# Layer 0's first key and query tiles projected by quarters of 256 features, between the modulation slabs

## What is computed

```python
m_lat = (cond_lat @ mod_w[i] + mod_b[i]).reshape(bsz, N_MOD, 1, dm)
m_ctx = (cond_ctx @ mod_w[i] + mod_b[i]).reshape(N_MOD, dm)
h_lat = x_lat * (1.0 + m_lat[:, 1]) + m_lat[:, 0]
h_ctx = x_ctx * (1.0 + m_ctx[1]) + m_ctx[0]
q, k, v = jnp.split(h @ w_qkv, cuts, axis=-1)     # layer 0
```

## Time and profile before

| what | value |
|---|---|
| median of the three runs | 2414.4 us |
| span of the profiled execution | 2413.2 us |
| time of the profiled execution outside its span | not given; the span is 1.2 us under the median |
| TensorE matmul busy | 2340.2 us (97%) |
| first projection matmul starts | 43.28 us |
| matmul of tile 3 starts | 69.19 us |
| moved by DMA | 310.94 MB, mean 129 GB/s |

### The profile page before, as it was taken

One profiled execution on the slowest core, in us unless ns is written; L12 is line 12 of the kernel. 1 busy time (PEld: TensorE's weight loads), 2 busy tenths in 40 slices (PEclk: granted clock), 3 DMA queues, 4 the chain that ended last, 5 costly groups with the idle time before them and its releaser, 6 DMA issues.

```text
span 2413.2 us, 35782 instructions
## 1 busy us (share of the span) xinstructions
PE 2340.2 (97%) x13872; PEld 1903.1 (79%) x13872; DVE 1696.3 (70%) x2583; ACT 1129.2 (47%) x1948; POOL 335.6 (14%) x269
## 2 busy tenths in 40 slices
PE   6999999999999989999999999899999999989998
PEld 3765888888888559888879877788888889848998
DVE  3376689988444777999875236768999845487875
ACT  3466643442442576434324444455434325386663
POOL 0000311111110003111112003422111102002110
PEclk9999999999999999999999999999999999999999
DMA  8621645557233113555563421043555645404664
GB/s 260 204 71 39 215 142 164 166 148 208 81 97 92 30 58 100 166 157 166 162 180 86 113 70 45 2 132 114 166 163 158 192 116 125 129 13 123 187 180 132
DMA packets 449420, 310.94 MB, mean 129 GB/s; under 512 B 11922, under 2 KB 404674, under 8 KB 448996
## 3 DMA queue, kind: packets, MB, share of 16 engines
q1 hardware_dynamic: 446480, 307.09, 43.2%
q10 hardware_dynamic: 2772, 1.56, 0.2%
HBM read 307.56 MB, written 1.05 MB: 128 GB/s over the span
## 4 chain that ended last, share of the span: by engine, by line
PE 85%; DVE 6%; ACT 4%; issue 2%; DMA 2%; ACTq 0%; SPq 0%; DVEq 0%
PE bank L1690 74%; PE bank L1973 2%; DMA slab_raw<-in_mod_w 2%; PE bank L1993 1%; PE bank L2037 1%; ACT p L793 1%; DVE slab_lo L1047 1%; DVE stat L1316 1%; ACT hb L610 1%; DVE q_part L1375 1%; PE bank L1749 1%; PE bank L1768 1%; ACT slab_hi L595 1%; ACT pt L805 1%; PE bank L2165 1%
## 5 line engine op out<-in xcount | busy, mean ns | idle before, releaser
L1690 PE MATMUL bank<-h_hi,slab_hi 128*128 128x512 f32 (+1 forms) x2416 | 841.9, 348 | 4.1 <-DVE h_lo L1112 2.5
L1690 PE MATMUL bank<-h_hi,slab_lo 128*128 128x512 f32 (+1 forms) x2416 | 828.9, 343 | 0.0
L1690 PE MATMUL bank<-h_lo,slab_hi 128*128 128x512 f32 (+1 forms) x2416 | 828.9, 343 | 0.0
L1047 DVE TENSOR_TENSOR slab_lo<-slab_raw,slab_hi 128x1024 fp32r<-128x1024 f32 (+1 forms) x388 | 526.2, 1357 | 296.1 <-ACT slab_hi L595 294.8
L595 ACT ACTIVATE slab_hi<-slab_raw 128x1024 fp32r<-128x1024 f32 (+1 forms) x388 | 400.8, 1034 | 303.8 <-PE bank L1690 228.0
L1690 PEld LDWEIGHTS bank<-h_hi,slab_hi 128*128 128x128 f32 x2416 | 458.0, 190 | 85.6 <-issue 19.8
L1690 PEld LDWEIGHTS bank<-h_hi,slab_lo 128*128 128x128 f32 x2416 | 458.0, 190 | 53.8
L1690 PEld LDWEIGHTS bank<-h_lo,slab_hi 128*128 128x128 f32 x2416 | 458.3, 190 | 53.3 <-issue 0.5
L1021 ACT ACTIVATE conv<-bank,prm 128x512 f32<-128x512 f32 (+1 forms) x176 | 127.7, 725 | 446.6 <-PE bank L1690 446.6
L1072 DVE SCALAR_TENSOR_TENSOR mod_sum<-slab_raw,cond_wide,mod_sum 128x512 f32<-128x512 f32 x420 | 316.5, 812 | 0.3 <-DMA slab_raw<-in_mod_w 0.2
L1690 PE MATMUL bank<-g_hi,slab_hi 128*128 128x512 f32 (+1 forms) x788 | 272.0, 345 | 0.0
(11 more groups left out here) (248 smaller groups left out, 2658.0 us busy)
## 6 DMA issues: line engine op xcount, KB each, us to landing
slab_raw<-in_ffn_w_up SPq DMA_DIRECT2D x176, 512.0 KB, 3.9
slab_raw<-in_mod_w SPq DMA_DIRECT2D x168, 512.0 KB, 4.6
slab_raw<-in_ffn_w_down SPq DMA_DIRECT2D x64, 512.0 KB, 3.6
slab_gap<-in_mod_w SPq DMA_DIRECT2D x24, 512.0 KB, 7.6
slab_raw<-in_ffn_w_down SPq DMA_DIRECT2D x32, 384.0 KB, 3.2
slab_raw<-in_b_w_qkv SPq DMA_DIRECT2D x24, 512.0 KB, 3.8
slab_raw<-in_c_w_in SPq DMA_DIRECT2D x24, 512.0 KB, 3.8
slab_raw<-in_d_w_qkv SPq DMA_DIRECT2D x24, 512.0 KB, 3.8
```

Of the source, the lines that this page charges most:

```text
L1047: nc.vector.tensor_tensor(wlo[slot][:, 0:w], raw[of][:, 0:w], whi[slot][:, 0:w].bitcast(f32), ALU.subtract).then_inc(s_lo, 1)
L1690: ins = mm(out, l, r, start=first and n == 0, stop=last and n == 2, skip_group_check=parted)
```

## The change

The 16 first modulation slabs are taken in another order: four slabs (two of shift, two of scale) that together give 256 features, then the next four. Each *quarter* f is turned, biased and made into a scale by itself, the tokens are loaded in four quarters of 256 features, and the first three dense slabs stand among the modulation slabs 4 to 6. TensorE then works through: slabs of quarter 0, slabs of quarter 1, projection of quarter 0 into tiles 0, 1 and 2, slabs of quarter 2, projection of quarter 1, and so on. Tile 2 is thus projected with tiles 0 and 1. On TensorE the table turns, `squares(0)`, part-1 slabs 16 to 19, `squares(1)`, and `turn(0)` follow behind that in their old sequence, without tile 2's projection among them. In the queue dense slab 4 now stands ahead of modulation slabs 16 to 19, where it stood behind them.

The new order of places is: mod 0 to 3, dense 0, mod 4, dense 1, mod 5, dense 2, mod 6 to 15, dense 3, dense 4, mod 16 to 19, dense 5, mod 20 to 23; from there it is as before.

```diff
+FIRST = 3
 def mod_items(part):
     i, g0, g1 = mod_groups(part)
+    if part == 0:
+        return [(0, g, f % 2, q) for f in range(PAIRS) for g in (f // 2, 2 + f // 2) for q in range(2)]
...
+    def add_first(ft):
+        add(("f", "a_w_qkv", qkv_tiles(0)[ft] * P, 0, 8))
     for m in range(16):
+        if m in (4, 5, 6):
+            add_first(m - 4)
         order.append(("mod", m))
...
             for ft in range(10):
-                add(("f", "a_w_qkv", qkv_tiles(0)[ft] * P, 0, 8))
+                if ft >= FIRST:
+                    add_first(ft)
                 owner.append("dve")
                 add_mods(1, mods_after("qkv", ft))
...
-                if place == 4:
+                if place == 2:
                     load_rows(slice(0, 2), s_rows)
-                if place == 8:
-                    load_tokens(slice(0, 2 * P), s_tok)
-                if place == 17:
-                    load_tokens(slice(2 * P, 4 * P), s_tok_2)
-                if place == 18:
-                    load_tokens(slice(4 * P, D), s_tok_3)
+                for f, at_place in enumerate((4, 9, 13, 17)):
+                    if place == at_place:
+                        load_tokens(slice(2 * P * f, 2 * P * f + 2 * P), s_tok[f])
...
-            splits_to(1)
             for pr in range(PAIRS):
...
                 for p in range(2):
                     modulate(0, p, pr)
+                if pr == 0:
+                    splits_to(FIRST - 1)
             splits_to(AHEAD)
...
+            def first_row_copy(f):
+                dve.wait_ge(s_mod_used, 4 * f + 4)
+                if f >= 2:
+                    dve.wait_ge(s_mod_t, f - 1)
+                nc.vector.tensor_copy(mod_row[:, first_half(f)], MOD_ACC[:, first_half(f)]).then_inc(s_mod_row, 1)
+            def first_scale(f):
+                dve.wait_ge(s_mod_t, f + 1)
+                of = MOD_T[:, 0:N_MOD * DT * 2].rearrange("p (b g s) -> p g b s", b=4, s=2)
+                for which in range(2):
+                    g, b = 2 * which + f // 2, slice(2 * (f % 2), 2 * (f % 2) + 2)
+                    k = DT * which + 2 * f
+                    bias_b = prm[:, k:k + 2]
+                    for s in range(2):
+                        ins = nc.vector.tensor_tensor(modT[0][:, k:k + 2, s], of[:, g, b, s], bias_b, ALU.add)
+                ins.then_inc(s_mod_in, 1)
+                dve.wait_ge(s_mod_in, f + 1)
+                nc.vector.tensor_scalar(coef[0][:, 0:2, 2 * f:2 * f + 2],
+                                        modT[0][:, DT + 2 * f:DT + 2 * f + 2, :].rearrange("p k s -> p s k"),
+                                        1.0, None, ALU.add).then_inc(s_first, 1)
...
-            mod_row_copy(0)
-            mod_evacuate(0, 0, 4, 0)
-            coefficients(0, mod_events(0, 0))
-            dve.wait_ge(s_coef, 1)
+            first_row_copy(0)
+            first_scale(0)
...
+            def first_turn(f):
+                pe.wait_ge(s_mod_row, f + 1)
+                if f >= 2:
+                    pe.wait_ge(s_mod_in, f - 1)
+                for b in (2 * (f % 2), 2 * (f % 2) + 1):
+                    ins = mm(MOD_T[:, 2 * GROUPS * b:2 * GROUPS * (b + 1)], mod_row[:, b * P:(b + 1) * P], sel,
+                             start=True, stop=True)
+                ins.then_inc(s_mod_t, 1)
...
                     if ft == 0:
+                        for f in range(PAIRS):
+                            if f + 1 < PAIRS:
+                                first_slabs(f + 1)
+                            if f == 0:
+                                pe.wait_ge(s_rows_v, 1)
+                                split_ready(n + FIRST - 1)
+                            pe.wait_ge(s_hlo, h_steps(0, 1, f) + 1)
+                            for k in (2 * f, 2 * f + 1):
+                                for j in range(FIRST):
...
+                        pe.wait_ge(s_mod_in, PAIRS)
+                        pe.wait_ge(s_rows_2, 16)
+                        turn_rows(6, 2, 6)
+                        turn_rows(7, 6, 8)
-                    elif ft >= 2:
+                    elif ft >= FIRST:
...
+            def first_slabs(f):
+                for m in range(4 * f, 4 * f + 4):
+                    mod_slab(0, m)
+                if f == 0:
+                    pe.wait_ge(s_lam_p, 1)
+                    mm(bank[5][:, 0:2], ones[0:HD, :], small[0:HD, 9:11], start=True, stop=True).then_inc(s_lam_d, 1)
+                    pe.wait_ge(s_rows, 16)
+                    turn_rows(2, 0, 2)
+                    first_turn(0)
+                pe.wait_ge(s_tok[f], 32)
+                turn_input(2 * f)
+                turn_input(2 * f + 1)
+                if f:
+                    first_turn(f)
```

More of the change, by code:

```diff
@@ L109, in mod_events @@
 def mod_events(i, part):
-    return part + 1 if i == 0 else i + 3
+    return PAIRS + part if i == 0 else PAIRS + i + 2
 def sum_step(m):
@@ L150, in make_plan @@
     for i in range(layers):
-        start["qkv", i] = (len(slabs), len(owner))
+        start["qkv", i] = (len(slabs), len(owner)) if i else (0, 0)
         if i == 0:
             for ft in range(10):
-                add(("f", "a_w_qkv", qkv_tiles(0)[ft] * P, 0, 8))
+                if ft >= FIRST:
+                    add_first(ft)
                 owner.append("dve")
@@ L326, in build_program @@
         s_free = {"act": sem("group_freed_act"), "dve": sem("group_freed_dve")}
[L327 to L330, removed]
+        s_cst, s_cond, s_rows, s_small, s_bias_in = (sem(n) for n in (
+            "consts_in", "cond_in", "rows_in", "small_in", "bias_in"))
+        s_tok = [sem(f"tokens_in{f}") for f in range(PAIRS)]
+        s_rows_2, s_rope, s_x0_odd, s_first = (sem(n) for n in (
+            "rows_in_2", "rope_tables_in", "input_turned_odd", "first_scale_ready"))
         s_cond_t, s_cond_a, s_rows_t, s_rows_v, s_tok_t = (sem(n) for n in (
@@ L347, in build_program @@
         s_kd, s_window = sem("keys_doubled"), sem("bias_masked")
-        s_lam_p, s_lam_d, s_lam_e, s_gains = (sem(n) for n in (
-            "lambda_products", "lambda_dots", "lambda_exps", "gains_ready"))
+        s_lam_p, s_lam_d, s_lam_e = (sem(n) for n in (
+            "lambda_products", "lambda_dots", "lambda_exps"))
         s_outz, s_outt, s_outv, s_out = sem("out_gained"), sem("out_transposed"), sem("out_normed"), sem("out_stored")
@@ L1546, in _ @@
                 dve.wait_ge(s_x0, 2 + pr)
+                dve.wait_ge(s_first, pr + 1)
                 if pr:
@@ L1550, in _ @@
                     ins = nc.vector.tensor_scalar(hb[1][:, k % 2, :], xn[:, k, CTX:T], coef[0][:, 1, k:k + 1],
-                                                  coef[0][:, 3, k:k + 1], ALU.mult, ALU.add)
+                                                  modT[0][:, k, 1:2], ALU.mult, ALU.add)
                 ins.then_inc(s_x1, 1)
-                if pr == 0:
-                    split(0)
                 for p in range(2):
@@ L1557, in _ @@
                 if pr == 0:
-                    split(1)
+                    splits_to(FIRST - 1)
             splits_to(AHEAD)
+            dve.wait_ge(s_lam_e, 1)
+            link(nc.vector.tensor_tensor(small[:, 13:14], small[:, 12:13], small[:, 11:12], ALU.subtract))
+            link(nc.vector.tensor_scalar(small[:, 13:14], small[:, 13:14], LAM_INIT, None, ALU.subtract))
             for b, c in enumerate((slice(R_LAYER, R_LAYER + NB), slice(R_LAYER + NB, R_LAYER * DEPTH))):
@@ L1741, in mod_slab @@
                 if m == 0 and part:
-                    pe.wait_ge(s_mod_row, part)
+                    pe.wait_ge(s_mod_row, PAIRS + part - 1)
+                if part == 0 and m in (8, 12):
+                    pe.wait_ge(s_mod_row, m // 4 - 1)
                 if m == 0 and part == 1:
@@ L1749, in mod_slab @@
                     ins = mm(MOD_ACC[TILE * j:TILE * j + TILE, NB // 2 * h:NB // 2 * h + NB // 2], cond_wide[:, z:z + TILE],
-                             raw[slot][:, NB // 2 * j:NB // 2 * j + NB // 2], start=g == g0 and q == 0,
-                             stop=g == g1 - 1 and q == 1)
+                             raw[slot][:, NB // 2 * j:NB // 2 * j + NB // 2],
+                             start=m % 4 == 0 if part == 0 else g == g0 and q == 0,
+                             stop=m % 4 == 3 if part == 0 else g == g1 - 1 and q == 1)
                 ins.then_inc(s_mod_used, 1)
@@ L1801, in keep_busy @@
             def keep_busy(part, times):
-                pe.wait_ge(s_mod_in, part)
+                pe.wait_ge(s_mod_in, PAIRS + part - 1)
                 for _ in range(times):
@@ L1863, in turn_input @@
             def turn_input(k):
-                if k >= 6:
-                    pe.wait_ge(s_x0, 3)
+                if k == 2:
+                    pe.wait_ge(s_lam_e, 1)
+                if k in (3, 4, 5):
+                    pe.wait_ge(s_x0, k - 2)
+                if k == 6:
                     pe.wait_ge(s_x0_odd, 1)
+                if k == 7:
+                    pe.wait_ge(s_x0, 4)
```

(15 more changed lines are left out.)

81 lines of the change are left out of this document (25 added, 56 removed).

## The result

The changed kernel's median is 2418.04 us (2415.38 to 2423.08, 11 runs), against 2411.41 us of the kernel before (2407.62 to 2415.91, 11 runs, which include the three shown above). The ratio is 1.0027, 95% interval 1.002 to 1.0035: 6.6 us slower. Put on record was 5.3 us slower (2419.7 us, range 2410.5 to 2427.5), with a chance of 0.50 for slower.

The account below looks back on a forecast made before the run. TensorE, its matmuls busy 97% of the span, was taken as the bound, so only the start could win. Tile 3's start, 72.5 + 2.0 - 69.2 = +5.3 us, added to the median gave 2419.7 us, 80% range 2410.5 to 2427.5.

Parts of the forecast that it names:

- First drain: Dense 2's load waits for dense 0's split, behind the first quarter's modulation; issued at 23.6, the stream stands 6.0 us.
- Second drain: Slab 12's load waits for slab 8's use behind quarter 0's projection; it lands at 44.9, not 40.8: 4.1 us more.
- End of the three tiles: When tiles 0, 1 and 2 are projected: slab 15 landed at 50.9, plus 10.8, gives 61.7 us.
- Rival 3: Clock stays low through the quarters because transfers chop TensorE's work: +11.5 us, 2425.9; chance 0.15.
- Third drain: Behind the three tiles, slab 19's load waits for dense 4's split behind tile 0's root; TensorE stands about 6 us.
- Low clock behind it: After TensorE's wait for slab 19 the clock falls to 0.50: 2.0 us charged, bounds 0 and 3.4.
- TensorE has no slack behind that would give a shift back.: Behind tile 3's start, TensorE is always busy, so none of the +5.3 us is regained.

Follow-up runs that it names:

- The one experiment against it: Changed kernel with each quarter's four modulation slabs used by TensorE one projection earlier: +7.7 us against the kernel before (1.0032).
- early split: Changed kernel with dense 0's split moved ahead of the first quarter's modulation on ScalarE and VectorE: +2.4 us against the kernel before (1.0008).
- both together: Changed kernel with dense 0 split early and slabs 16 to 19 queued ahead of dense 4 again: -0.5 us against the kernel before (1.0001).
- matmuls in the wait: Changed kernel with seven extra unused matmuls between modulation slabs 18 and 19: +6.9 us against the kernel before (1.0023).
- the experiment without the third drain: Changed kernel with modulation slabs 16 to 19 queued ahead of dense slab 4 again: +1.9 us against the kernel before (1.0009).
- changed again: Changed kernel run once more, unchanged, for a second profile: +6.6 us against the kernel before (1.0023).
- before again: Kernel before run once more, unchanged, for a second profile: +0.1 us against the kernel before (0.9998).
- the one with dense 4 first: Kernel before with only dense slab 4 queued ahead of modulation slabs 16 to 19: +5.5 us against the kernel before (1.0026).

## Why the prediction was right, and where its terms were off

**First drain.** It came as worked out: dense 2 was issued at 23.73 (put: 23.6), and ScalarE splits it from 27.35 (put: landed at 27.3). Slab 7 was used at 33.11, not from 31.8. Undone, this drain gave 4.2 us with three tiles and 9.9 with two.

**Second drain.** It is there: quarter 0 ends at 40.97 (40.7), all at the high clock. Slab 15 was used at 53.30 and 51.65, not 50.9: the transfers behind the hole ran at 323 GB/s (44 to 54 us, first profile), where the sum had 350. The sum also charged the hole in full. The one experiment against it won nothing (+7.7), but that one moved the wait and did not take it away, so what this hole costs by itself is not shown.

**End of the three tiles.** This is the term that was mis-sized: 61.7 put, 66.7 and 65.0 measured. Of that, 0.8 to 2.4 us is slab 15. The other part is the clock. From slab 15's use to the tiles' end the prediction had 10.8 us; it was 13.4 in both profiles of the changed kernel, and 10.7 in each of the four experiments with this order in which the clock did not fall (third drain, early split, both together, matmuls in the wait). The granted clock from 54 to 58 us in the changed kernel, and from 52 to 59 in the experiment without the third drain:

```profile
54.00:56.00 2.00, 2.00 (x13) 2.00 (x11) 0.42 (x1) 0.60 (x1) 0.00 (x0) 0.50 1.08 321
56.00:58.00 2.00, 2.00 (x7) 1.71 (x8) 1.28 (x7) 0.11 (x1) 0.00 (x0) 0.50 1.08 330
```

```profile
52.00:59.00 7.00, 6.80 (x42) 5.31 (x35) 4.32 (x12) 3.79 (x6) 0.00 (x0) 1.00 1.08 327
```

In the changed kernel TensorE was busy 0.28 of the 2 us from 50 to 52 and 1.06 of those from 52 to 54, waiting for slabs 14 and 15. But waits alone do not tell when the clock falls: it fell in the changed kernel's second profile behind waits of 1.61 and 0.80 us for these slabs, and not with the early split behind 2.61 and 0.93. Two of the experiments (third drain, matmuls in the wait) are the changed kernel itself up to this place, and there it did not fall; so it is not a fixed cost of the change but one that some executions pay. Rival 3 had given such a fall 6.2 us in quarters 0 and 2, with a chance of 0.15; 2.7 us of it came.

**Third drain.** Slab 19 was used 9.5 and 9.6 us after the tiles' end (9.2 put), by the steps that were given. It is shown twice, by taking it out (4.7 us) and by putting it into the old kernel (5.5 us).

**Low clock behind it.** It was put at 2.0 and measured as 2.3 us by the profiles with and without matmuls in the wait. The Trainium skill (TensorE: Matmul & The Clock Gate, Loop structure matters more than you think) says that a long wait for a DMA between matmuls drops the clock; the row of 76 to 80 us at 0.50 agrees. The Trainium skill's fit for GpSimd's path (DMA: Bandwidth & Descriptors, Anatomy of one DMA) gives an estimate of 3.2 us for such a slab; through SyncE's queue it took 3.6 us for dense 2 and 4.12 for slab 19, so the rows were the better source.

**"TensorE has no slack behind that would give a shift back."** The times do not bear this out, and that hid the term that was mis-sized. Attention starts 10.2 us later (means of two and three profiles), near twice the forecast of 5.3, but the median is only 6.6 us higher. Another 0.35 us of the difference lies outside the span. From attention to the end the changed kernel took 2269.1 and 2268.5 us, the one before 2273.0, 2269.5 and 2272.9. The difference of the means is 3.0 us and goes with the clock: from 140 to 2400 us the granted clock was at 0.50 for 17.1 and 13.7 us, against 23.9, 13.7 and 23.9. (A last fall, in the final 8 to 11 us of every profile, is left out.) One of the falls comes at attention's start. The kernel before has it in its first profile and not in its second:

```profile
138.00:160.00 22.00, 21.30 (x114) 11.77 (x113) 17.84 (x50) 14.29 (x42) 0.00 (x0) 0.84 0.18 48
```

```profile
138.00:160.00 22.00, 20.67 (x124) 11.58 (x124) 19.32 (x56) 16.11 (x48) 0.00 (x0) 1.00 0.16 48
```

That the falls set the difference is read from 14 profiles, not shown by an experiment, and the means rest on few executions. Taken alone, the two profiles nearest to their medians (changed again, before again) differ by 10.0 us at attention and by only 1.0 us behind it. So where a typical execution loses the rest of the shift stays open. The executions without a profile bear it out in part only: among the 29 of the kernel before that stood beside one group of experiments, the longer ones had the lower mean clock (correlation 0.59), but those at the same mean clock, 0.992, still lie between 2406.5 and 2412.6 us.

So the forecast's sign and mechanism held, and its size was partly luck: in the profiles the tiles' end came 3 to 5 us later than put, and between the shift at attention and the median some 3.5 us are missing, the other way. The forecast in us (2419.7) was also helped by its base: it stood on a median of three runs, 2414.4, where eleven runs gave 2411.4. On that base the forecast would have been 2416.7, against 2418.0 measured.

**What became of the 16 us of matmuls that the change puts under the transfers.** The prediction set the same state of the kernel before at 65.3 us (tile 2's end at 68.1 less 2.8 us of other work) and expected the tiles to end 3 to 4 us ahead of it. They ended at 66.7 and 65.0: the overlap won nothing by then. Where the clock did not fall it won the 2 to 3 us (62.4, 63.2), and without the first hole 6.6 (58.7). What is left is given back at slab 19. Of the versions that were run, two tiles instead of three with one split moved is the only one that is clearly faster than the kernel before.

## What to carry to other kernels

When loads share a ring of buffers in one queue, an entry that is inserted decides which consumer each later load waits for; write down for each place the instruction that frees its buffer and what stands ahead of that on its engine. Taking one wait away shows only what the next one allows: here slab 23 stood behind slab 19. Before two phases are overlapped, see which work ran beside a later chain: here tile 2's projection, before it was moved forward, ran beside the split and the load of the slabs that come next.

## What was not expected of the hardware

The same kernel on the same chip spent 13.7 us at the low clock between layer 0's projections and 2400 us in one execution and 23.9 us in another, and the stretch from attention to the end was 3.4 us longer in the latter. Over 14 profiles of ten kernels that are the same from there on, that stretch was 2267.2 and 2267.3 us with 10.2 us of low clock, 2268.2 to 2269.5 with 13.7, 2269.1 and 2269.5 with 17.1, 2269.4 and 2270.4 with 20.5, and 2272.3 to 2273.0 with 23.9: about 0.4 us for each us of low clock. Whether the old order makes the long case likelier (three of its four profiles, the one with dense 4 first among them, none of ten others) stays open.
